# A two-block decoder kernel: who takes the low parts of 18 weight slabs in the stage of the recurrence

## The reference

```python
r = sigmoid(einsum(ub, wa) + ba)
i = sigmoid(einsum(ub, wx) + bx)
log_a = -RGLRU_C * r * softplus(-lam)
a = exp(log_a)
beta = sqrt(maximum(-expm1(2.0 * log_a), 0.0))
_, h = associative_scan(_linear_combine, (a, beta * (i * u)), axis=1, reverse=reverse)
...
y_a = (h_fwd + h_bwd) * gelu(g_lru)
gates = sigmoid(z + b_gate)
merged = gates[:, :, 0] * y_a + gates[:, :, 1] * y_b
x = x + merged @ w_out
```

## Time and profile before

| | us |
|---|---|
| median of 3 runs | 1547.47 |
| lowest, highest | 1546.45, 1548.66 |
| the profiled execution's own time | 1548.28 |
| its span, first to last instruction | 1546.5 |
| TensorE busy in the span | 1448.2 |
| VectorE busy | 881.1 |
| ScalarE busy | 638.3 |
| GpSimd busy | 1.9 |

### The profile page before, as it was taken

How to read it: one execution, slowest core, us unless ns; L and a number is a source line. 1 busy time by engine, 2 the same in 40 slices (tenths; PEclk the granted TensorE clock), 3 DMA queues, 4 the chain that set the end, 5 groups by cost and what they waited for, 6 DMA issues and landing times.

```text
span 1546.5 us, 17781 instructions
## 1 busy us (share of the span) xinstructions
PE 1448.2 (94%) x7272; PEld 1166.9 (75%) x7272; DVE 881.1 (57%) x1267; ACT 638.3 (41%) x994; POOL 1.9 (0%) x7
## 2 busy tenths in 40 slices
PE   6997899998999999999899999978899999999997
PEld 6876577777778888888687777756678888888886
DVE  5775564566544445364647877578874443443445
ACT  4445465333222222123425667778743321222232
POOL 0000000000000000000000000000000000000000
PEclk9998899999999999999899999989999999999998
DMA  4211222222133323233131111122233332333323
GB/s 157 87 65 42 92 91 64 85 93 82 60 109 96 98 94 108 84 96 106 43 109 55 52 45 56 55 68 68 68 109 96 96 98 93 96 97 108 92 86 109
DMA packets 36561, 131.64 MB, mean 85 GB/s; under 512 B 4432, under 2 KB 4560, under 8 KB 36224
## 3 DMA queue, kind: packets, MB, share of 16 engines
q1 hardware_dynamic: 36128, 127.16, 26.4%
q0 software_dynamic: 352, 3.34, 0.6%
HBM read 128.39 MB, written 2.10 MB: 84 GB/s over the span
## 4 chain that ended last, share of the span: by engine, by line
PE 69%; DVE 16%; ACT 11%; issue 3%; DMA 1%; SPq 0%; DVEq 0%; ACTq 0%
PE gp L1351 20%; PE gp L1353 20%; PE gp L1352 20%; DVE w_lo L783 2%; PE mp L1527 1%; ACT arena L706 1%; PE mp L1538 1%; ACT w_hi L414 1%; DVE arena L1006 1%; PE mp L1499 1%; DVE arena L1013 1%; ACT a_hi L441 1%; ACT arena L563 1%; PE mp L1380 1%; ACT arena L710 1%
## 5 line engine op out<-in xcount | busy, mean ns | idle before, releaser
L1351 PE MATMUL gp<-a_hi,w_hi 128*128 128x512 f32 x1120 | 443.8, 396 | 14.2 <-DVE arena L1244 13.0
L1352 PE MATMUL gp<-a_lo,w_hi 128*128 128x512 f32 x1120 | 439.0, 392 | 0.0
L1353 PE MATMUL gp<-a_hi,w_lo 128*128 128x512 f32 x1120 | 438.3, 391 | 0.0
L783 DVE TENSOR_TENSOR w_lo<-raw,w_hi 128x1024 fp32r<-128x1024 f32 x232 | 283.5, 1223 | 168.1 <-ACT w_hi L414 166.9
L414 ACT ACTIVATE w_hi<-raw 128x1024 fp32r<-128x1024 f32 x232 | 243.3, 1052 | 197.3 <-PE gp L1353 105.1
L1351 PEld LDWEIGHTS gp<-a_hi,w_hi 128*128 128x128 f32 x1120 | 212.2, 189 | 66.5 <-DVE w_lo L783 16.5
L1353 PEld LDWEIGHTS gp<-a_hi,w_lo 128*128 128x128 f32 x1120 | 212.1, 189 | 45.1
L1352 PEld LDWEIGHTS gp<-a_lo,w_hi 128*128 128x128 f32 x1120 | 212.2, 189 | 42.6
L1351 PE MATMUL gp<-h_hi,w_hi 128*128 128x512 f32 x576 | 224.9, 390 | 8.9 <-DVE h_lo L817 3.5
L1353 PE MATMUL gp<-h_hi,w_lo 128*128 128x512 f32 x576 | 224.1, 389 | 0.0
L1352 PE MATMUL gp<-h_lo,w_hi 128*128 128x512 f32 x576 | 224.1, 389 | 0.0
(11 more groups left out here) (236 smaller groups left out, 1438.5 us busy)
## 6 DMA issues: line engine op xcount, KB each, us to landing
raw<-slabs SPq DMA_DIRECT2D x232, 512.0 KB, 3.5
arena<-x_in SPq DMA_DIRECT2D x4, 512.0 KB, 6.2
arena<-x_in POOLq DMA_DIRECT2D x1, 2048.0 KB, 8.2
out_t<-arena SPq DMA_DIRECT2D x8, 256.0 KB, 2.1
arena<-bias POOLq DMA_DIRECT2D x1, 1024.0 KB, 5.9
arena<-s5b SPq DMA_DIRECT2D x1, 512.0 KB, 9.1
arena<-s5c SPq DMA_DIRECT2D x1, 512.0 KB, 10.0
par<-params SPq DMA_DIRECT2D x1, 232.0 KB, 2.6
```

The costliest lines, as they stand in the source:

```text
L783: TT(w_lo[:, n % RING, :], raw[:, n % RAW, :], w_hi[:, n % RING, :].bitcast(F32), ALU.subtract).then_inc(w_lo_ready, 1)
L1351: pe.matmul(dst, hi, x_hi(t), start=t == 0, stop=False)
L1352: pe.matmul(dst, hi, x_lo(t), start=False, stop=False)
L1353: ins = pe.matmul(dst, lo, x_hi(t), start=False, stop=t == tiles - 1)
```

## The change

GpSimd gets a loop over `BY_POOL`, the slabs 138 to 155, and makes their `w_lo` with the subtraction that VectorE had. It waits for `w_hi` of the slab, and for `w_lo` of the slab before, so that the count `w_lo_ready` rises in the order of the slabs. VectorE's `split` does nothing for these slabs, and its first one after them, slab 156, waits until GpSimd's last is counted.

```diff
+        BY_POOL = range(SLAB["mix"] + AHEAD, SLAB["out2"])
...
             pool.dma_start(nd8, nd2).then_inc(s_nd, 16)
+
+            for n in BY_POOL:
+                pool.wait_ge(w_hi_ready, n + 1)
+                pool.wait_ge(w_lo_ready, n)
+                pool.tensor_tensor(w_lo[:, n % RING, :], raw[:, n % RAW, :], w_hi[:, n % RING, :].bitcast(F32),
+                                   ALU.subtract).then_inc(w_lo_ready, 1)
...
             def split(n):

-                if n >= NSLAB:
+                if n >= NSLAB or n in BY_POOL:
                     return
                 dve.wait_ge(w_hi_ready, n + 1)
+                if n == BY_POOL.stop:
+                    dve.wait_ge(w_lo_ready, n)
                 TT(w_lo[:, n % RING, :], raw[:, n % RAW, :], w_hi[:, n % RING, :].bitcast(F32),
                    ALU.subtract).then_inc(w_lo_ready, 1)
```

## The result

The changed kernel takes 1563.04 us (median of 4 runs, 1561.69 to 1565.51); the kernel before, run beside it on the same chip, 1547.12 (4 runs). The ratio is 1.010, with an interval of 1.0087 to 1.0113: 15.9 us slower. The profiled execution took 1563.31 us with a span of 1561.5, 15.0 more than the span before.

The account below looks back on a forecast made before the run. It took the loop over t between ScalarE and VectorE to bound the recurrence stage. Turns +40.0, hidden detour -18.9 and tail -1.1 sum to +20 us, 1567 us from 1547.5, with a range of 1533 to 1580.

Parts of the forecast that it names:

- What bounds the stage: Recurrence stage, 152.0 us: bound by the loop over t between ScalarE and VectorE, not by TensorE; even steps 14.6 us.
- the detour: Odd steps wait 6.3 us more for a slab's late w_lo, its DMA and w_hi; hiding this gives -18.9 us.
- The tail: Behind the last scan, where VectorE runs back to back, one w_lo fewer gives -1.1 us.
- The stage's end: Recurrence stage said to end at 1133.49 us, where TensorE starts the first slab of out2.
- The turns: In the recurrence, GpSimd's subtraction and VectorE's two-input instructions take turns reading SBUF; chance 0.56, likeliest 1567 us.
- How often: 17 of the 18 GpSimd instructions fall into VectorE's recurrence; slab 138 is free.
- The size of a hit: Each GpSimd instruction meeting the recurrence costs VectorE p less 0.09 us; 17 x (2.44 - 0.09) = +40.0 us.
- p: Length of one GpSimd two-input subtraction of 128x1024: taken as 2.44 us, bounded by 1.22 and 3.66.
- TensorE's clock: Granted clock may fall in more places of the stage; costed at nothing, at worst 1 to 2 us in a step.
- Rival 1: GpSimd reads beside VectorE in the recurrence and holds nothing up: -13.7 us, 1534; chance 0.27.
- Rival 2: Neither engine blocks, each slows the other; VectorE loses half the overlap: +2 to +7 us, 1552; chance 0.09.
- Rival 3: GpSimd gets in only when VectorE pauses, so the recurrence keeps its length: +6 us, 1553; chance 0.08.

Follow-up runs that it names:

- the events alone: Changed kernel, but each GpSimd instruction only clears one column and raises the count; 1528.60 us, ratio 0.9882.
- the half size: Changed kernel, but each of the 18 GpSimd subtractions covers 512 columns in place of 1024; 1542.57 us, ratio 0.997.
- the memset: Changed kernel, but GpSimd clears all 1024 columns of each slab's low part in place of subtracting, so it reads nothing; 1531.14 us, ratio 0.9891.
- the held variant: Changed kernel, but GpSimd's first slab of each step t waits for the sum of that step's recurrence, all 18 subtractions kept; 1553.13 us, ratio 1.0036.
- the experiment with 24 in a row: Kernel before, plus 24 useless two-input GpSimd subtractions of 128x1024 back to back in the first block's MLP; 1575.09 us, ratio 1.0178.
- the three slabs alone: Changed kernel, but GpSimd makes w_lo only for slabs 140, 145 and 150, VectorE all others; 1537.10 us, ratio 0.9936.

## Why the prediction came out as it did

- **What bounds the stage** held. The loop over t is the bound, even steps without a hold are 14.6 us, and the detour is worth 18.9 us in all: with the events alone every step is at 14.6 to 14.7 and the kernel 18.7 us faster. The tail gave its 1.1 us: from the last L1274 to the matmul behind the last `h_lo` it was 15.3 us, and is 14.2.
- **The stage's end** I named wrongly. The matmul at 1133.49 us in the earlier trace rows is not the first of `out2`; that slab starts at 1127.03, and 1133.49 is its eighth chunk, which waits for the last `h_lo` (the row of 1127.03 stands below the list). The 152 us thus hold 20 7/8 slabs, some 114 us of TensorE's work in place of 109. The argument that TensorE isn't the bound stands, and no term rests on the 109.
- **The turns** held, as the timelines, the half size, the memset and the held variant show together. Which instruction is held is the one that comes second, as the Trainium skill says (SBUF — State Buffer, "Who interferes with whom"): the trace agrees, with 2.09, 2.10 and 1.96 us in t = 3, where GpSimd's row starts ahead of each held one. It goes both ways: the third GpSimd row starts while L1283 runs, and is 0.57 us longer than alone.
- **How often**: 17 hits, one in t = 0, three in each of t = 1, 3 and 5, two in each of t = 2, 4 and 6, one in t = 7. It came out so: the first seven steps are 16.7, 20.7, 18.7, 20.8, 18.8, 20.8 and 18.7 us, and slab 138 at 981.55 is free.
- **The size of a hit** is the term that was off. I took p = 2.44 us and a hit of p - 0.09 = 2.35, which makes +40.0. A subtraction that meets nobody takes 2.39 us (slab 138), the shortest 2.34, so p was good. But of those 2.39 us VectorE is held only some 2.07 (from the steps and t = 3: 2.09, 2.10, 1.96); in the other 0.3 of the row VectorE runs. The forecast's step that a two-input instruction loses all of p was too much by that. 17 x 2.07 = 35.2, and 35.2 - 18.9 - 1.1 = +15.2 us, against +15.0 in the spans and +15.9 in the medians. The steps were to be 19 and 22 us, and are 18.7 and 20.7; the matmul that I called `out2`'s first was to start near 1153, and starts at 1148.02. The Trainium skill (GPSIMD Engine Reference, "Elementwise — side-by-side cycle accounting") gave an estimate of 2.25 us for p; the trace has 6% more, and as a hit is shorter than p, its sum of +17 came nearer by two errors that partly cancel.
- **TensorE's clock** I had costed at nothing, with a loss in reserve. It fell in the stage, 0.92 to 0.89, and TensorE was busy 3.5 us longer there; but the steps and the tail make up the whole of the stage's 14.9 us, so none of that was on the path.
- **Rival 1** (free reading, 1534) is ruled out for the subtraction, and is what happens with an instruction that reads nothing: 1531. Its path for an odd step, worked out with the memset's 0.95 us in place of 2.44, gives 15.2 us, and the memset's odd steps are 15.3. **Rival 2** (mutual slowing by half of the overlap) is ruled out by the clean rows beside the long ones: L1283 at 1.19, L1277 at 0.69. **Rival 3** (behind the recurrence) was put at +6; made on purpose it gives +5.4.
- **That an idle engine's work costs nothing** I argued again in the experiment with 24 in a row, and was wrong by 24 us; the forecast of this change had not depended on it.

The first matmul of `out2` in the kernel before:

```profile
1127.03 0.39 PE L1351 MATMUL gp<-h_hi,w_hi 128*128 128x512 f32 x1
```

## What to carry to other kernels

Before work is given to GpSimd, list what VectorE does at the moment when GpSimd will start, not how busy VectorE is on the average: an instruction with two inputs in SBUF, or a clamp like the one above, was held here for up to nearly the whole of GpSimd's, once for each GpSimd instruction that reads. Against a saving at the critical place stands (number of meetings) x (hold). The split pays where the meetings fall into VectorE's own pauses, or where, as with the three slabs alone, the saving is larger than the few holds. Where a late engine causes a detour, moving its own instruction forward can be cheaper than moving it to another engine: three early `w_lo` on VectorE bring -13.4 us, three on GpSimd -10.2, all 18 on GpSimd +15.9.

## What the runs showed of the hardware

- GpSimd's subtraction of 128x1024 fp32 takes 2.34 to 2.39 us alone and holds VectorE 2.0 to 2.1; of 128x512, 1.28 and 0.94 to 1.13. VectorE needs 1.22 and 0.69 for the same.
- A GpSimd copy with one input holds VectorE too (0.69 to 1.30 us beside a copy of 128x896, which takes 0.94 alone). A memset of 128x1024, 0.95 us, does not.
- VectorE's one-input clamp of 128x1024, which reads at twice the rate, is held as the two-input ones are (0.69 to 1.43). A VectorE instruction with one input from PSUM and one from SBUF is not held: 0.68 us in the midst of the 24, and 0.69 between the held products of the run with all 18 behind the recurrence. How a single input at the lower rate fares, no run here shows.
- ScalarE's copies (1.04 us) and TensorE's matmuls (0.39 at a granted clock of 1.00, from 1088.3 to 1090.7 us of the changed kernel) keep their times beside GpSimd.
- Where both engines have such instructions ready, they go one for one: 24 and 24 in 70 us, however short VectorE's are.
